# Writing out TensorE's program for the 14 looped head pairs of a hybrid RWKV-7 / gated-MLP layer

## What is computed

```
def step(S, inp):
    r_t, w_t, k_t, v_t, kk_t, b_t = inp
    sa = einsum('bhij,bhj->bhi', S, kk_t)
    S = S * w_t[:, :, None, :] - sa[..., None] * b_t[:, :, None, :] + v_t[..., None] * k_t[:, :, None, :]
    return S, einsum('bhij,bhj->bhi', S, r_t)

for d in range(2):
    s_ctx, yc = wkv_scan(zeros, *dir_inputs(tc, d), reverse=(d == 1))
    _, yx = wkv_scan(s_ctx, *dir_inputs(tx, d), reverse=(d == 1))
y = ys_x[0] + ys_x[1]      # then a per-head norm, a bonus term and a gate
```

## Time and profile before

| | |
|---|---|
| time, median of 3 runs | 3207.3 us (3206.77 to 3211.29) |
| profiled execution: its time, its span | 3207.55 us, 3205.8 us |
| TensorE matmul busy | 2982.5 us, 93% |
| TensorE weight load busy | 2250.8 us, 70% |
| VectorE, ScalarE, GpSimd busy | 1745.8, 951.8, 434.1 us |
| pair 0 begins, pair 14 begins, pair 15 begins (first L703) | 256.27, 1685.71, 1775.53 us |
| mean granted TensorE clock | 0.964 of full speed |

### The profile page before, as it was taken

The page is one execution under the profiler, slowest core; times in us unless marked ns, Lnnn a source line. Parts: engine busy times, 40 slices in busy tenths (PEclk is TensorE's granted clock), DMA queues, the critical chain, the costliest instruction groups (busy, mean ns, idle before and its releaser), DMA issues.

```text
span 3205.8 us, 70945 instructions
## 1 busy us (share of the span) xinstructions
PE 2982.5 (93%) x28320; PEld 2250.8 (70%) x28320; DVE 1745.8 (54%) x3292; ACT 951.8 (30%) x1635; POOL 434.1 (14%) x580
## 2 busy tenths in 40 slices
PE   5899999998999999999999899999999999999997
PEld 1245555555555555555556569999989999999997
DVE  1135545564456545564456345444348888886444
ACT  1122212222122222222122143333344444443333
POOL 0001100111111110111011102000002333331000
PEclk8899999999999999999999999999999999999999
DMA  7512222121222222122222244555444555554553
GB/s 313 240 71 98 79 73 89 61 100 61 87 79 74 87 74 82 59 100 74 74 80 87 108 165 152 182 183 183 165 169 144 181 181 181 181 182 162 178 180 134
DMA packets 66106, 412.81 MB, mean 129 GB/s; under 512 B 8176, under 2 KB 10864, under 8 KB 25328
## 3 DMA queue, kind: packets, MB, share of 16 engines
q1 hardware_dynamic: 65136, 407.51, 35.4%
q0 software_dynamic: 768, 2.10, 0.2%
HBM read 405.38 MB, written 4.19 MB: 128 GB/s over the span
## 4 chain that ended last, share of the span: by engine, by line
PE 82%; DVE 9%; issue 4%; DMA 2%; ACT 2%; POOL 0%; SPq 0%; DVEq 0%; ACTq 0%; POOLq 0%; PEldq 0%
PE PB L651 16%; PE Q L899 6%; PE Q L900 6%; PE Q L904 6%; PE PB L899 4%; PE PB L900 4%; PE PB L904 4%; PE CH L904 3%; PE CH L900 3%; PE CH L899 3%; DVE arena L1402 2%; PE Q L767 2%; PE Q L784 2%; DMA ring<-w_mod_dram 2%; PE PB L636 2%
## 5 line engine op out<-in xcount | busy, mean ns | idle before, releaser
L651 PE MATMUL PB<-hT,ring 128*128 128x512 f32 (+1 forms) x1536 | 686.6, 556 | 5.4 <-PEq L640 5.4
L1585 DVE TENSOR_TENSOR w_lo_r<-ring,w_hi_r 128x1536 fp32r<-128x1536 f32 (+3 forms) x178 | 387.5, 2177 | 268.9 <-ACT w_hi_r L1194 268.9
L1194 ACT ACTIVATE w_hi_r<-ring 128x2048 fp32r<-128x2048 f32 (+2 forms) x178 | 325.7, 1830 | 452.4 <-PE Q L904 211.4
L651 PEld LDWEIGHTS PB<-hT,ring 128*128 128x128 f32 x1536 | 251.9, 189 | 139.6 <-issue 95.9
L900 PE MATMUL PB<-hT_r,w_hi_r 128*128 128x256 f32 x832 | 204.6, 285 | 0.0
L1745 DVE TENSOR_TENSOR w_lo_r<-ring,w_hi_r 128x1408 fp32r<-128x1408 f32 x62 | 101.2, 1633 | 148.0 <-ACT w_hi_r L1308 148.0
L899 PE MATMUL PB<-hT_r,w_hi_r 128*128 128x256 f32 x704 | 175.7, 289 | 4.7 <-DVE hT_r L1672 4.7
L899 PE MATMUL Q<-ff_hi_r,w_hi_r 128*128 128x256 f32 x704 | 175.6, 288 | 1.8 <-ACT w_hi_r L1308 1.8
L900 PE MATMUL Q<-ff_lo_r,w_hi_r 128*128 128x256 f32 x704 | 172.9, 284 | 0.0
L899 PE MATMUL CH<-hT_r,w_hi_r 128*128 128x256 f32 x704 | 170.9, 283 | 0.0
L900 PE MATMUL CH<-hT_r,w_hi_r 128*128 128x256 f32 x704 | 170.9, 283 | 0.0
(11 more groups left out here) (262 smaller groups left out, 6028.3 us busy)
## 6 DMA issues: line engine op xcount, KB each, us to landing
ring<-w_mod_dram SPq DMA_DIRECT2D x96, 1024.0 KB, 5.0
ring<-w_up_dram SPq DMA_DIRECT2D x88, 1024.0 KB, 4.8
ring<-w_rkv_dram SPq DMA_DIRECT2D x48, 1024.0 KB, 4.9
ring<-w_down_dram SPq DMA_DIRECT2D x64, 704.0 KB, 4.0
ring<-w_ga_dram SPq DMA_DIRECT2D x16, 1024.0 KB, 4.8
ring<-w_gb_dram SPq DMA_DIRECT2D x16, 1024.0 KB, 4.8
ring<-w_pa_dram SPq DMA_DIRECT2D x16, 1024.0 KB, 4.8
ring<-w_out_dram SPq DMA_DIRECT2D x16, 1024.0 KB, 4.8
```

The costliest lines, as they stand in the source:

```text
L651: last = mm(PB[slot % 2][:, 0:cols], tile(n, kt), hT[:, kt, 0:cols], start=(kt == 0), stop=(kt == KT - 1))
L1194: f(w_hi_r[:, r % 2, 0:n], ring[:, r, 0:n], ACT.Copy).then_inc(hi_rdy, 1)
L1585: tt(w_lo_r[:, r, 0:n], ring[:, r, 0:n], as_f32(w_hi_r[:, r % 2, 0:n]), ALU.subtract).then_inc(lo_rdy, 1)
```

## The change

TensorE's loop over pairs 0 to 13 is written out: the same `body`, called 14 times with a number in place of the register. No other engine's program is touched, and the order of TensorE's matmuls is the same.

```
--- before.py
+++ after.py
@@ -876,7 +876,7 @@
             project(0, 2)
             project(1, 0)
             project(1, 1, 0, 6)
-            with pe.Fori(0, PAIRS - 2) as i:
+            for i in range(PAIRS - 2):
                 body(i, 2)
             body(PAIRS - 2, 1)
             body(PAIRS - 1, 0)
```

## The result

With TensorE's 14 pairs written out the kernel takes 3150.28 us (median of 4 runs, 3148.07 to 3152.6) against 3207.03 us before: ratio 0.9822, 95% interval 0.9805 to 0.9839, some 57 us less. The forecast was 3161.7 in a range of 3136 to 3175.

A forecast was written before the change was run, and what follows sets the result against it. TensorE, busy 93% of the span, was taken as the bound, standing still at its pair loop's jumps. Removing thirteen jumps gains 72.7 us, returning low clock costs 27, net 45.7: 3161.7 us, range 3136 to 3175.

The forecast's parts named there:

- Thirteen jumps removed, priced by start times: TensorE's pair loop, pairs 0 to 13: idle time and half clock at the jumps go, 72.7 us gained.
- Nobody late at the seam: From L869 to L725: no other engine's wait replaces the jump; ScalarE's readout is done 1.5 us before L725.
- Registers at nothing: Register counting in TensorE's pair loop: no gain taken from removing it, bounds nothing and 0.2 us a pair.
- Fetch at nothing: Instruction fetch of TensorE's written-out pairs: straight code fetches no more than the loop does, priced at nothing.
- Low stretches behind L767: Half clock after the pause before the first L767: returns in 9 of pairs 1 to 14, 3.0 us each, 27 us lost.
- rival 1: Pauses before L767 stay harmless, at most 4 low stretches: 3134.7 to 3146.7 us, chance 0.19.
- rival 2: All 14 pairs fall to the lower clock behind the pause before L767: 3176.7 us, chance 0.05.
- Rival 3: Before L703, another engine's wait (VectorE's L1555) replaces the jump: only 5 us gained, 3202 us, chance 0.03.
- Rivals 4 and 5: Idle time before L703 has another cause, no change, chance 0.01; straight code starves instruction supply, up to 3590 us, chance 0.03.

The follow-up runs named there:

- the doubled body: Against the kernel before, TensorE's pair loop kept but with two pairs in its body and 7 passes, 6 jumps: 3162.57 us, ratio 0.9855.
- loops of one pass: Against the kernel with the change, each of TensorE's 14 pairs put inside its own loop that runs once: 3154.61 us, ratio 0.9852 to the kernel before.
- the jump moved: TensorE's pair loop kept, its seam behind L710 instead of L869, 12 jumps: 3171.04 us, ratio 0.9895 to the kernel before.
- the four with another up projection: The change, with TensorE's up-projection loop body lengthened to three, four, five or seven groups: 3150.70, 3147.03, 3158.28 and 3147.33 us.
- A0 moved as well: The change with W0 ahead of the first L767, plus the second low-rank product moved behind L791 in the first level: 3125.14 us, ratio 0.9754.

## Why the prediction came out as it did

The mechanism was right, the sign and the range too; the forecast was 11 us too high. In the profiled executions it was 3161.9 against 3148.07. By its own steps:

- **Thirteen jumps removed, priced by start times.** Seam predicted 0.63, measured 0.63. Pair in straight code predicted 96.72, measured 96.47. Of the 0.25 us 0.2 are the pause before the first L767: taken as 1.97 us from the one straight sample, it is 1.76 or 1.77 in most pairs. 13 x 0.25 = 3.2 us of the miss.
- **Nobody late at the seam.** Right; L725 starts 2.57 us behind L703 in all 14 pairs.
- **Registers at nothing.** Right to 0.1 us a pair, shown by the second pairs of the doubled body; the loops of one pass, built to show it, do not. The 0.2 us between the two L767 that I had as a bound is there in loops (6.43 us) and not in straight code (6.25), and outside that stretch it is partly made up.
- **Fetch at nothing.** Right for the time. But I had expected 189 packets or a few more, and there are 159. The extra ones go with the jumps: 30 at 13 jumps, 27 at 12 (the jump moved, 186), 15 at 6 (two bodies, 174). That they are packets loaded ahead past the loop's end and dropped is my reading and not shown.
- **Low stretches behind L767.** The step that was mis-sized. Predicted: 9 of the 14 pairs from 1 to 14, 3.0 us each, 27 us. Measured: 8, none in pair 14, and four of them half as long. Pairs 0 to 13 take 1370.9 us in all (253.50 to 1624.38), 20.3 above 14 x 96.47, of which 0.6 are pair 9's without any half clock. That is 6.7 us of the miss. I had also kept pair 0's low stretch as not touched by the change; in the profiled execution it wasn't there, 2.9 us. Five other kernels here have the same straight pairs (loops of one pass, and the four with another up projection). Of their 15 such pauses 6, 5, 9, 5 and 9 brought the clock down, with this one 42 of 90; pair 0's did in two of the five. Their pairs 0 to 13 take 12.6 to 20.7 us above 14 x 96.47, never 27. So both factors were too high, two in three for the share and 3.0 us for the loss of each (some 2.5 here), and that 8 came so near the forecast 9 was in part luck.
- **The rest.** Pair 0 starts 2.8 us earlier, and from pair 14 on it takes 1.8 us longer (1521.9 against 1520.1), together 0.9.

3.2 + 6.7 + 2.9 + 0.9 = 13.7 of the 13.8 us. Neither rival 1 (at most 4 low stretches) nor rival 2 (all 14) came; there were 8. Rival 3, another engine's wait in the jump's place, did not come; built on purpose, with a wait of 2.8 us at the seam, it cost all of the gain (ratio 1.0003, 0.9993 to 1.0013) and not all but 5 us. A pause without a jump can bring the low clock as well; why the last 5 us were missing too was not followed up. Rivals 4 and 5 fell: the seam is 0.63 us, and no new pause appeared: the "issue" of 6.1 us in 12 times ahead of L835 stands where VectorE was named before, and L835's pauses in the pairs are 23.3 us in all, against 24.5.

The nominal 108 ns of a compare-and-branch in the Trainium skill ("Advanced Engine Details and Errata", Control Flow Timing) is near what the exit shows (67 to 83 ns) and half of a short jump (0.21 us); it says nothing of a long one. The rule in "Runtime: NRT & Kernel Launch" of the Trainium skill, Instruction fetch mechanics, that a jump out of the two pages held must fetch first, agrees with the two prices and with the packets. Its figures do not give the limit: bodies of 1586 instructions, more than two of its pages of 256, still jump in 0.21 us, and bodies of 1982, fewer than the 2048 that it gives TensorE, pay 3.6. The step measured here lies between 1586 and 1982 instructions.

Open: what decides whether a pause of 1.8 us brings the clock down. Of the 15 such pauses after, which follow the same work, 8 did. Their length does not decide: pauses of 1.75 us were followed by half clock, and one of 2.01 and one of 2.40 us (five and four groups in the up projection) were not.

## What to carry to other kernels

Look at the compare-and-branch rows of a loop, not at its average: a loop body that the engine can't hold (the limit lies between 1586 and 1982 instructions of TensorE here) stops its sequencer for 3.3 to 3.9 us at every jump, while VectorE's loop of the same passes pays 0.06. Write it out, shorten it, or put its seam where long matmuls that wait for nothing are queued; where the loop is left, or where straight code follows it, the trace of before already holds a sample of the result. And read every pause of TensorE twice, once as idle time and once as the half clock behind it: filling 1.8 us of pause in 15 pairs with 0.95 us of work was worth some 5 us of idle time and 18 to 20 us of clock.

## What was not expected of the hardware

- The price of a jump has two values, and nothing between was seen: 0.21 us up to 1586 instructions, 3.3 to 3.9 us from 1982 on, the same at 2280, at 2774 and at twice 2280.
- Low stretches are 3.4 or 6.8 us long behind these pauses, and a pause as short as 1.66 us can be followed by one. When one pause has had its low stretch, the next often has none: with pauses at both places, the clock fell once a pair in most pairs, behind the one or the other.
- The same program can differ by 26 us between executions in this way (3141.88 to 3168.29 in the loops of one pass, clock 0.973 to 0.964); with the pause filled the executions lie between 3124.68 and 3131.17, but with A0 moved as well again between 3119.55 and 3135.58.
